# An eight-tile prologue rebuilt: order of transfers, paired conditioning blocks, gate rows as two float32 products side by side

## Chip, cores and metric

One Trainium2 chip, one of its cores. The metric is the device time of the program in microseconds (us), median of its runs. The kernel is written in Bass: every engine has an instruction list of its own and the engines meet at semaphores (`wait_ge`, `then_inc`), so the order on each engine is the order in the code.

## The reference

One layer over x of 1024 tokens by 1024 columns, all float32. What matters here is how it begins:

```
mod = silu(c) @ w_ada + b_ada
shift, scale, gate = split(mod, 3)
h = x * (1 + scale) + shift
proj = h @ w_in + b_in
```

`proj` has 6664 columns: q, k, v, z of eight stick-breaking attention heads of 64, q, k, v, o, z of four mLSTM heads of 128, eight columns of input and forget gates, and two merge gates of 1024 columns. Attention and mLSTM follow, both are projected, merged with the sigmoids of the merge gates, multiplied by `w_out`, and `LayerNorm(alpha * x + (1 + gate) * y)` is the output.

## The kernel before

Products are made in float32r, with each float32 operand split in a high part and a rest (`hH`, `hL`; `wH`, `wL`) and three products for each (`split_product`, L614): high by high, high by low, low by high. h lies transposed in SBUF, eight tiles of 128 columns by 1024 tokens. A *job* (`project`, L621) is 128 output columns for all tokens: eight tiles by two halves of 512 tokens by three products, 48 in all. Five jobs (0 to 4) belong to the prologue, the rest follow in a fixed order under the attention and mLSTM work of four iterations. After the prologue the tensor engine (PE) works through one list to the end.

**The prologue** makes h tile by tile and, as each tile is there, adds its share to jobs 0, 1 and 2 at once: job 0 is the eight gate columns, 1 and 2 are q and k of the first pair of heads. For tile d:

- SyncE (SP) loads x's columns (half a MiB in rows of 512 bytes, L453) and two blocks of `w_ada`, shift and scale (half a MiB each, L457), into one of `A_BUFS` = 3 buffers, and at the first tiles the chunks of `w_in` for the jobs (L443). Seven small loads of parameters stand ahead of all of them (L434, L435).
- VectorE (DVE) sums the eight row blocks of `w_ada` times `silu(c)` (`ada_rows`, L1323: L1331, L1334, L1337).
- The PE sums over the partitions with a product by ones (`ada_columns`, L650; line L655 in the profile); DVE adds the bias (`mod_columns`, L1362).
- The PE transposes x's eight blocks of 128 by 128 (`turn_x`, L659; L667). ScalarE (ACT) makes h from them with scale and shift (`shifted`, L937: L944, two halves) and its high part (L948); DVE makes the rest (`low_h`, L1358).
- The PE makes 18 products for the tile (`tile_of`, L671; lines L617 to L619): six for job 0, whose weights have 8 columns, six for job 1, six for job 2.

The PE's order is: turn of tile d, products of tile d - 1 for jobs 0 and 1, column product of tile d + 1, products of tile d - 1 for job 2. Jobs 3 and 4 follow as ordinary jobs (L639). Job 3 uses the same two PSUM banks as job 1, so its first product waits until ACT has copied out the first half of job 1.

The results of job 0 are copied by ACT (`bias_copy`, L959 to L961), and then SP copies its two groups of rows to four places each, with four small transfers for `r_f` (L470) and four for `r_i` (L472). ACT's exponential (L993) waits for all eight; DVE's scans over the gates (L1388 to L1408) follow, with the splits of weight chunks 9 and on between them (L1343). GpSimd (POOL) only clears buffers in the prologue.

## Time and profile before

| | us |
|---|---|
| median of three runs | 962.69 (962.66 to 962.82) |
| the profiled execution, its own time | 964.36 |
| its span, first to last instruction | 962.6 |
| PE busy | 931.1 (97%) |
| VectorE busy | 616.4 (64%) |
| ScalarE busy | 440.4 (46%) |
| GpSimd busy | 165.5 (17%) |

The span is what the profile's views divide; the run's own time lies 1.7 us above it. Busy time of the PE counts a matmul from its start to its modelled end, so neighbours overlap: how fast the PE works is seen from the distance between starts. Times in the rows are us from the span's start unless they are marked ns.

### The profile page before, as it was taken

To read this page: it belongs to the slowest core of one execution; us is meant where nothing else is said; L and a number is where in the kernel's file an instruction comes from. 1 tells how busy PE (TensorE), PEld (TensorE's weight loads), DVE (VectorE), ACT (ScalarE), POOL (GpSimd) and SP (SyncE) were. 2 spreads that over 40 slices of the span, in tenths; PEclk is the share of its full clock that TensorE was granted. 3 is DMA by queue.
4 is the path that set the end of the run, shared out by engine and by line. 5 is a ranking of instruction groups with operands and counts; after the bars stand their busy time and mean duration, and the time that the engine had idled before them with its cause. 6 is when DMAs were issued, how large, how long until landed. Compare 5 with 4: busy or idle time off the path is not lost.

```text
span 962.6 us, 12901 instructions
## 1 busy us (share of the span) xinstructions
PE 931.1 (97%) x4965; PEld 759.7 (79%) x4965; DVE 616.4 (64%) x1112; ACT 440.4 (46%) x717; POOL 165.5 (17%) x114
## 2 busy tenths in 40 slices
PE   2999999999999999999999999999999999999996
PEld 1677878888878888788888888888888888878885
DVE  4756886755976647976649967534653333345996
ACT  2454566553666544575544665425743222242100
POOL 1010232220223230322311322211100000001200
PEclk9999999999999999999999999999999999999999
DMA  9941211112201022111112111127612212215232
GB/s 228 291 99 48 67 35 39 35 36 67 77 23 45 23 55 78 43 45 34 33 44 89 33 35 34 43 55 237 211 45 67 53 46 53 88 44 186 91 129 87
DMA packets 99560, 73.95 MB, mean 77 GB/s; under 512 B 4616, under 2 KB 90760, under 8 KB 99500
## 3 DMA queue, kind: packets, MB, share of 16 engines
q1 hardware_dynamic: 94828, 58.44, 22.7%
q0 software_dynamic: 2368, 8.41, 2.6%
q10 hardware_dynamic: 2304, 6.29, 1.8%
q8 instruction: 39, 0.64, 0.3%
q14 instruction: 21, 0.17, 0.1%
HBM read 64.59 MB, written 8.40 MB: 76 GB/s over the span
## 4 chain that ended last, share of the span: by engine, by line
PE 89%; DVE 4%; ACT 2%; SPq 2%; DMA 2%; issue 1%; DVEq 0%; ACTq 0%
PE bank L639 44%; PE bank L619 10%; PE bank L617 10%; PE bank L618 10%; PE bank L758 4%; PE bank L746 3%; PE bank L733 2%; DMA a_raw<-in_w_ada 2%; PE bank L716 2%; DVE rem L1503 1%; PE bank L735 1%; PE bank L734 1%; SPq L457 1%; PE bank L781 1%; PE bank L783 1%
## 5 line engine op out<-in xcount | busy, mean ns | idle before, releaser
L639 PE MATMUL bank<-hH,wH 128*128 128x512 f32 x688 | 271.1, 394 | 0.6 <-DVE wL L1343 0.6
L639 PE MATMUL bank<-hL,wH 128*128 128x512 f32 x688 | 271.2, 394 | 0.0
L639 PE MATMUL bank<-hH,wL 128*128 128x512 f32 x688 | 271.1, 394 | 0.0
L577 POOL TENSOR_TENSOR ez<-ez,rem 128x512 f32<-128x512 f32 x72 | 134.5, 1881 | 396.8 <-DVE rem L1503 396.8
L1343 DVE SCALAR_TENSOR_TENSOR wL<-w_raw,wH 128x512 fp32r<-128x512 f32 x116 | 99.3, 860 | 109.2 <-ACT wH L920 107.9
L639 PEld LDWEIGHTS bank<-hH,wH 128*128 128x128 f32 x688 | 129.3, 188 | 30.3 <-DVE wL L1343 2.1
L639 PEld LDWEIGHTS bank<-hH,wL 128*128 128x128 f32 x688 | 129.3, 188 | 28.8 <-issue 2.9
L639 PEld LDWEIGHTS bank<-hL,wH 128*128 128x128 f32 x688 | 129.2, 188 | 28.8 <-issue 2.9
L1503 DVE TENSOR_TENSOR_SCAN rem<-rem,ones 128x512 f32<-128x512 f32 (+2 forms) x96 | 99.9, 1093 | 35.1 <-ACT rem L1020 35.1
L920 ACT ACTIVATE wH<-w_raw 128x512 fp32r<-128x512 f32 x116 | 72.5, 627 | 104.3 <-PE bank L619 71.1
L1008 ACT ACTIVATE ez<-bank 128x512 f32<-128x512 f32 x72 | 39.1, 596 | 101.1 <-PE bank L735 101.1
L618 PE MATMUL bank<-hL,wH 128*128 128x512 f32 x144 | 56.2, 390 | 0.0
L617 PE MATMUL bank<-hH,wH 128*128 128x512 f32 x144 | 56.2, 390 | 0.0
L619 PE MATMUL bank<-hH,wL 128*128 128x512 f32 x144 | 56.0, 389 | 0.0
L606 POOL TENSOR_TENSOR yL<-yT,yH 128x1024 fp32r<-128x1024 f32 x4 | 9.6, 2402 | 207.5 <-ACT yH L1272 207.5
L1016 ACT ACTIVATE rem<-ez 128x512 f32<-128x512 f32 x72 | 41.4, 625 | 7.7 <-DVE y_stage L1510 6.1
L1020 ACT ACTIVATE rem<-rem 128x512 f32<-128x512 f32 x72 | 41.1, 621 | 0.0
L1027 ACT ACTIVATE at<-bank 128x512 f32<-128x512 f32 x72 | 38.7, 592 | 3.3 <-PE bank L746 3.3
L617 PE MATMUL bank<-hH,yH 128*128 128x512 f32 x96 | 38.5, 401 | 0.0
L618 PE MATMUL bank<-hL,yH 128*128 128x512 f32 x96 | 38.1, 396 | 0.0
L619 PE MATMUL bank<-hH,yL 128*128 128x512 f32 x96 | 38.0, 396 | 0.0
L746 PE MATMUL bank<-ident,ez 128*128 128x128 f32 x288 | 37.2, 272 | 0.0
(241 smaller groups left out, 1499.6 us busy)
## 6 DMA issues: line engine op xcount, KB each, us to landing
w_raw<-in_w_in SPq DMA_DIRECT2D x104, 256.0 KB, 2.9
a_raw<-in_w_ada SPq DMA_DIRECT2D x16, 512.0 KB, 7.3
x_rows<-in_x SPq DMA_DIRECT2D x8, 512.0 KB, 6.4
raw<-in_w_ada POOLq DMA_DIRECT2D x8, 512.0 KB, 4.8
x_in<-in_x SPq DMA_DIRECT2D x8, 512.0 KB, 4.2
out_y<-res SPq DMA_DIRECT2D x7, 512.0 KB, 2.9
raw<-in_w_out SPq DMA_DIRECT2D x10, 256.0 KB, 4.5
m_w<-bm_scratch ACTq DMA_DIRECT2D x4, 512.0 KB, 3.5
```

Source lines behind the costliest of these rows:

```text
L577: g.tensor_tensor(e, e, r, ALU.mult).then_inc(a_done[h], 1)
L617: t.matmul(ps, aH, bH, start=k == 0, stop=False)
L618: t.matmul(ps, aH, bL, start=False, stop=False)
L619: return t.matmul(ps, aL, bH, start=False, stop=k == kt - 1)
L639: ins = t.matmul(banks(number)[half][:], w, a, start=(r == 0), stop=(r == JOB_MM // 2 - 1))
L746: ins = t.transpose(z_ps[h][:, b * P:(b + 1) * P], ez[s % 2][h][:, b * P:(b + 1) * P], ident[:])
L920: a.activation(wH[:, slot, :, 0:width], w_raw[:, slot, :, 0:width], ACT.Copy, scale=scale)\
L1008: a.activation(ez[s % 2][h][:], z_ps[h][:], ACT.Exp).then_inc(ex_done[h], 1)
L1016: a.activation(rem[s % 2][h][:], ez[s % 2][h][:], ACT.Ln, bias=1.0).then_inc(ln_done[h], 1)
L1020: a.activation(r, r, ACT.Exp, scale=-1.0).then_inc(rem_done[h], 1)
L1343: v.scalar_tensor_tensor(out=wL[:, slot, :, 0:width], in0=w_raw[:, slot, :, 0:width], scalar=scale, in1=wH[:, slot, :, 0:width], op0=ALU.m ...
L1503: v.tensor_tensor_scan(back, back, ones[:, 0:1].to_broadcast((P, hi - lo)), first, ALU.mult, ALU.min).then_inc(scan_done[h], 1)
```

## The change

The prologue alone is touched, up to the copy of job 0.

- **Order of loads.** SP first issues two small loads (c and `b_ada`), then for each block the conditioning weights, then x. The other five small loads go out from ACT, ahead of its table load. The first three chunks of `w_in` follow block 0, the next three block 3. The parameters are transposed in two parts.
- **Pairs.** Tiles 4 and 5 and tiles 6 and 7 are each one block: two pieces of `w_ada` (half of the rows each) of 256 columns, so rows of 1 KB, and one load of x of 256 columns. There are four buffers for conditioning weights; the fourth lies in the place of `next_v` and `next_g`.
- **Sums ahead.** DVE's order is written out by hand: the sums of the next block are begun before the low part of the tile before.
- **Turns ahead.** The PE transposes x of tile d + 2 behind the products of tile d; column products have places of their own.
- **Gate rows.** Job 0 is no longer three split products. It is one float32 product per half straight from `h_raw`, with unsplit weights (`w_if`), half 0 into partitions 0 to 7 and half 1 into partitions 32 to 39 of one bank. DVE moves half 1 to partitions 0 to 7 before ACT adds the bias.
- **Row copies.** The four loads of `r_i` are issued by ACT between the copies of job 0 and those of job 1; the four of `r_f` stay with SP.

```diff
@@ -127,9 +127,28 @@
-A_BUFS = 3
+A_BUFS = 4
+BLOCKS = [[0], [1], [2], [3], [4, 5], [6, 7]]
+BLOCK_OF = [b for b, tiles in enumerate(BLOCKS) for _ in tiles]
...
+def pro_slot(g):
...
+    return (g // PRO_K) * (PRO_K - 1) + g % PRO_K - 1
...
+def ada_pieces(b):
...
+    if b < 4:
+        return [(b, 0, KT)]
+    return [(2 * b - 4 + part, part * KT // 2, (part + 1) * KT // 2) for part in range(2)]
...
+def ada_freed(number):
...
+    return [KT * b + hi for b in range(len(BLOCKS)) for n, _, hi in ada_pieces(b) if n == number - A_BUFS][0]
@@ -280,13 +300,14 @@
-        a_raw = pt("a_raw", [P, A_BUFS, KT, 2, P])
-        a_acc = pt("a_acc", [P, 2, 2, 2, P])
+        a_raw = [pt(f"a_raw{n}", [P, KT * 2 * P]) for n in range(A_BUFS - 1)] + [next_vg]
+        a_acc = pt("a_acc", [P, 2, 2, 2, 2 * P])
...
+        w_if = pt("w_if", [P, KT, 2 * NH])
@@ -424,17 +458,8 @@
...
+            sp.dma_start(prm[ROW_C:ROW_C + KT, :], c[0].rearrange("(t p) -> t p", p=P)).then_inc(c_in, 16)
+            sp.dma_start(prm[ROW_ADA:ROW_ADA + 3 * KT, :], b_ada[0].rearrange("(t p) -> t p", p=P)).then_inc(c_in, 16)
@@ -448,19 +473,17 @@
-            for d in range(KT):
-                cols_d = slice(d * P, (d + 1) * P)
-                sp.dma_start(x_rows[:, :, cols_d], x_v[:, :, cols_d]).then_inc(x_cols_in[d], 16)
-                if d >= A_BUFS:
-                    sp.wait_ge(ada_used, KT * (d - A_BUFS + 1))
-                for what in range(2):
-                    sp.dma_start(a_raw[:, d % A_BUFS, :, what], w_ada_w[:, :, what, cols_d])\
-                        .then_inc(a_in[d % A_BUFS], 16)
-                if d == 0:
-                    for g in range(3):
-                        pro_load(g)
-                elif d < 4:
-                    pro_load(d + 2)
+            for b, tiles in enumerate(BLOCKS):
+                cols_b = slice(tiles[0] * P, (tiles[-1] + 1) * P)
+                for number, lo, hi in ada_pieces(b):
+                    if number >= A_BUFS:
+                        sp.wait_ge(ada_used, ada_freed(number))
+                    for what in range(2):
+                        sp.dma_start(ada_piece(number, lo, hi)[:, :, what], w_ada_w[:, lo:hi, what, cols_b])\
+                            .then_inc(a_in[number % A_BUFS], 16)
+                sp.dma_start(x_rows[:, :, cols_b], x_v[:, :, cols_b]).then_inc(x_cols_in[b], 16)
+                for g in {0: range(3), 3: range(3, PRO_CHUNKS)}.get(b, ()):
+                    pro_load(g)
@@ -468,8 +491,6 @@
-            for q in range(4):
-                sp.dma_start(r_i[32 * q:32 * q + NH, :], r_if[0:NH, :]).then_inc(rows_in, 16)
@@ -644,42 +665,61 @@
-            pe.wait_ge(params_in, 16 * 7)
-            t.transpose(misc_ps[0][:, 0:P], prm[:], ident[:]).then_inc(m_filled[0], 1)
...
-            def ada_columns(d):
...
-                pe.wait_ge(ada_summed, d + 1)
-                pe.wait_ge(m_drained[0], d + 1)
+            pe.wait_ge(c_in, 16 * 2)
+            r = slice(ROW_ADA, P)
+            t.transpose(misc_ps[0][:, 0:P - ROW_ADA], prm[r, :], ident[r, r]).then_inc(m_filled[0], 1)
+            pe.wait_ge(params_in, 16 * 5)
+            r = slice(0, ROW_ADA)
+            t.transpose(misc_ps[2][:, P:P + ROW_ADA], prm[r, :], ident[r, r]).then_inc(params_turned, 1)
...
+            def ada_columns(b):
...
+                pe.wait_ge(ada_summed, b + 1)
+                if b:
+                    pe.wait_ge(mod_done, b)
+                tiles = len(BLOCKS[b])
...
+                    for n in range(tiles):
+                        ins = t.matmul(ada_ps[:, tiles * what + n:tiles * what + n + 1],
+                                       a_acc[:, b % 2, 0, what, n * P:(n + 1) * P], ones[:, 0:1],
+                                       start=True, stop=True)
...
-                pe.wait_ge(x_cols_in[d], 16)
+                pe.wait_ge(x_cols_in[BLOCK_OF[d]], 16)
...
-                    if n == 0:
-                        pe.wait_ge(mod_done, 2 * d + 2)
-                    elif d:
-                        pe.wait_ge(m_drained[n], d)
+                    if d + 1 - n:
+                        pe.wait_ge(m_drained[n], d + 1 - n)
...
-            def tile_of(k, first, last):
+            def gate_rows(d):
...
+                for n in range(2):
+                    pe.wait_ge(m_drained[n], d + 2 - n)
+                if d % 4 == 0:
+                    pe.wait_ge(wL_done, PRO_K * (d // 4) + 1)
+                for half in range(2):
+                    ins = t.matmul(pro_ps[0][half], w_if[:, d], h_raw[:, d % 2, halves(half)], start=d == 0,
+                                   stop=d == KT - 1, skip_group_check=True)
+                    if d == KT - 1:
+                        ins.then_inc(filled[half], 1)
+                    elif half:
+                        ins.then_inc(if_used, 1)
...
+            def tile_of(k, n):
...
+                g = PRO_K * (k // 4) + n
...
-                    pe.wait_ge(wL_done, PRO_K * (k // 4 + 1))
-                for n in range(first, last):
-                    w = [z[:, PRO_K * (k // 4) + n, k % 4, 0:P if n else 2 * NH] for z in (w_proH, w_proL)]
-                    for half in range(2):
-                        ins = split_product(pro_ps[n][half], w, (hH[:, k, halves(half)], hL[:, k, halves(half)]),
-                                            k, KT)
-                        if k == KT - 1:
-                            ins.then_inc(filled[half], 1)
+                    pe.wait_ge(wL_done, g + 1)
+                w = [z[:, pro_slot(g), k % 4] for z in (w_proH, w_proL)]
+                for half in range(2):
+                    ins = split_product(pro_ps[n][half], w, (hH[:, k, halves(half)], hL[:, k, halves(half)]), k, KT)
+                    if k == KT - 1:
+                        ins.then_inc(filled[half], 1)
@@ -696,16 +736,21 @@
+            turn_x(0)
...
+            turn_x(1)
...
-                turn_x(d)
-                if d:
-                    tile_of(d - 1, 0, PRO_K - 1)
-                if d + 1 < KT:
-                    ada_columns(d + 1)
-                if d:
-                    tile_of(d - 1, PRO_K - 1, PRO_K)
-            tile_of(KT - 1, 0, PRO_K)
+                if d in (1, 2, 5):
+                    ada_columns(min(d + 1, 5))
+                gate_rows(d)
+                if d == 0:
+                    ada_columns(1)
+                tile_of(d, 1)
+                if d == 3:
+                    ada_columns(4)
+                tile_of(d, 2)
+                if d + 2 < KT:
+                    turn_x(d + 2)
@@ -906,6 +951,13 @@
+            bi = b_in[0]
+            for row, src in [(ROW_B, bi[0:OFF_IF]), (ROW_GSB, bi[OFF_GSB:OFF_GSB + 2 * D]), (ROW_CB, conv_b[0]),
+                             (ROW_NG, ml_norm_g[0])]:
+                src = src.rearrange("(t p) -> t p", p=P)
+                act.dma_start(prm[row:row + src.shape[0], :], src).then_inc(params_in, 16)
+            act.dma_start(prm[ROW_CW:ROW_CW + 4 * KT, :], conv_w[0].rearrange("j (t p) -> (j t) p", p=P))\
+                .then_inc(params_in, 16)
@@ -936,8 +990,9 @@
-                act.wait_ge(mod_done, 2 * d + 2)
+                act.wait_ge(mod_done, BLOCK_OF[d] + 1)
...
+                    act.wait_ge(if_used, d - 1)
@@ -977,8 +1034,10 @@
-                        bias_copy(r_if[0:2 * NH, halves(half)], half, n,
-                                  r_bias[0:2 * NH, :], pro_ps[0][half])
+                        else:
+                            act.wait_ge(if_moved, 1)
+                        rows = r_if[0:2 * NH, halves(half)]
+                        bias_copy(rows, half, n, r_bias[0:2 * NH, :], rows if half else pro_ps[0][half])
@@ -988,6 +1047,11 @@
+                if n == 0:
+                    for half in range(2):
+                        act.wait_ge(drained[half], 1)
+                    for q in range(4):
+                        act.dma_start(r_i[32 * q:32 * q + NH, :], r_if[0:NH, :]).then_inc(rows_in, 16)
@@ -1306,36 +1370,45 @@
+            r = slice(ROW_ADA, P)
...
-            def ada_rows(d):
...
+            def other_columns():
+                r = slice(0, ROW_ADA)
+                dve.wait_ge(params_turned, 1)
+                link(v.tensor_copy(cols[:, r], misc_ps[2][:, P:P + ROW_ADA]))
+                link(v.tensor_scalar(cols[:, 0:4], cols[:, 0:4], SB_SCALE, None, ALU.mult))
+                v.tensor_scalar(ncols[:, r], cols[:, r], -1.0, None, ALU.mult).then_inc(params_made, 1)
+                dve.wait_ge(params_made, 1)
...
+            def ada_rows(b, lo, hi):
...
+                if lo == 0 and b > 1:
+                    dve.wait_ge(ada_done, b - 1)
+                for k in range(lo, hi):
+                    for number, first, _ in ada_pieces(b):
+                        if k == first:
+                            dve.wait_ge(a_in[number % A_BUFS], 32 * (number // A_BUFS + 1))
+                    acc, row = ada_sum(b, k % 2), ada_row(b, k)
...
+                if hi == KT:
+                    dve.wait_ge(ada_used, KT * (b + 1))
+                    v.tensor_tensor(ada_sum(b, 0), ada_sum(b, 0), ada_sum(b, 1), ALU.add).then_inc(ada_summed, 1)
@@ -1359,27 +1434,48 @@
-            def mod_columns(d):
-                dve.wait_ge(ada_done, d + 1)
...
-            for d in range(KT):
-                ada_rows(d)
-                if d:
-                    low_h(d - 1)
-                mod_columns(d)
-                if d == 0:
-                    for g in range(3):
-                        pro_split(g)
-                elif d < 4:
-                    pro_split(d + 2)
-            low_h(KT - 1)
+            def mod_columns(b):
+                dve.wait_ge(ada_done, b + 1)
+                first, tiles = BLOCKS[b][0], len(BLOCKS[b])
...
+            other_columns()
+            ada_rows(0, 0, KT)
+            mod_columns(0)
+            for g in range(3):
+                pro_split(g)
+            ada_rows(1, 0, KT // 2)
+            low_h(0)
+            ada_rows(1, KT // 2, KT)
+            ada_rows(2, 0, KT // 4)
+            mod_columns(1)
+            ada_rows(2, KT // 4, KT)
+            low_h(1)
+            mod_columns(2)
+            ada_rows(3, 0, KT)
+            low_h(2)
+            mod_columns(3)
+            ada_rows(4, 0, KT // 2)
+            low_h(3)
+            ada_rows(4, KT // 2, KT)
+            for g in range(3, PRO_CHUNKS):
+                pro_split(g)
+            mod_columns(4)
+            ada_rows(5, 0, KT // 2)
+            low_h(4)
+            ada_rows(5, KT // 2, KT)
+            low_h(5)
+            mod_columns(5)
+            low_h(6)
+            low_h(7)
...
+            dve.wait_ge(filled[1], 1)
+            dve.wait_ge(rows_zero, 5)
+            v.tensor_copy(r_if[0:2 * NH, halves(1)], pro_ps[0][1]).then_inc(if_moved, 1)
```

## Rows read from the trace of the kernel before

**Rows 1.** The page: busy time by engine, and the chain's shares.

```profile
PE 931.1 (97%) x4965; PEld 759.7 (79%) x4965; DVE 616.4 (64%) x1112; ACT 440.4 (46%) x717; POOL 165.5 (17%) x114
...
PE 89%; DVE 4%; ACT 2%; SPq 2%; DMA 2%; issue 1%; DVEq 0%; ACTq 0%
```

**Rows 2.** Stretches: length, PE, PEld, DVE, ACT, POOL busy, granted clock, DMA share, GB/s.

```profile
30.00:40.00 10.00, 9.85 (x54) 6.86 (x52) 7.03 (x19) 5.54 (x7) 0.00 (x0) 1.00 1.17 291
...
40.20:43.60 3.40, 1.88 (x11) 1.56 (x11) 2.80 (x7) 0.00 (x0) 0.00 (x0) 1.00 1.11 286
...
43.60:47.05 3.45, 3.45 (x14) 2.24 (x13) 3.31 (x9) 1.92 (x3) 0.00 (x0) 0.51 1.12 296
...
870.00:880.00 10.00, 10.00 (x45) 8.02 (x44) 4.97 (x9) 5.07 (x7) 4.35 (x2) 1.00 0.97 336
```

**Rows 3.** The chain in order of time: start, length, what.

```profile
29.97 8.32 DMA a_raw<-in_w_ada
...
51.05 0.88 PE bank L667 x8
...
76.09 1.07 ACT r_e L993
```

**Rows 4.** Instructions in order of time: PE, idle time before in brackets.

```profile
41.82 0.61 PE L655 MATMUL bank<-ones,a_acc 128*128 128x1 f32 x4 [1.52 <-DVE a_acc L1337]
...
54.55 0.50 PE L655 MATMUL bank<-ones,a_acc 128*128 128x1 f32 x4
...
60.06 0.50 PE L655 MATMUL bank<-ones,a_acc 128*128 128x1 f32 x4
...
68.35 0.40 PE L617 MATMUL bank<-hH,w_proH 128*128 128x512 f32 x1
...
70.91 0.40 PE L619 MATMUL bank<-hH,w_proL 128*128 128x512 f32 x1
...
71.15 0.39 PE L639 MATMUL bank<-hH,wH 128*128 128x512 f32 x1
...
85.52 0.50 PE L639 MATMUL bank<-hH,wH 128*128 128x512 f32 x1 [0.58 <-DVE wL L1343]
```

**Rows 5.** Instructions in order of time: SyncE, VectorE and ScalarE in the prologue.

```profile
1.27 0.31 SPq L434 DMA_DIRECT2D prm<-in_b_ada  x1
...
3.48 0.43 SPq L453 DMA_DIRECT2D x_rows<-in_x  x1
...
11.43 0.61 DVE L1331 TENSOR_SCALAR a_acc<-a_raw,silu_c 128x256 f32<-128x256 f32 x2 [4.28 <-DMA a_raw<-in_w_ada]
...
66.40 1.89 DVE L1343 SCALAR_TENSOR_TENSOR wL<-w_raw,wH 128x512 fp32r<-128x512 f32 x3
...
67.94 1.28 ACT L961 ACTIVATE r_if<-bank,r_bias 8x512 f32<-8x512 f32 x2 [1.16 <-PE bank L619]
...
69.25 1.39 ACT L961 ACTIVATE next_q<-bank,cols 128x512 f32<-128x512 f32 x2
...
71.92 2.44 SPq L472 DMA_DIRECT2D r_i<-r_if  x4
```

**Rows 6.** Transfers between 870 and 880 us.

```profile
DMA packets 1160, 3.36 MB, mean 336 GB/s; under 512 B 128, under 2 KB 128, under 8 KB 1159
```

**Rows 7.** The chain in order of time: groups of products in two other places.

```profile
129.68 1.06 PE bank L716 x8
...
130.75 1.02 PE bank L758 x16
...
131.77 0.43 PE bank L733 x2
...
863.15 1.72 PE bank L877 x4
```

**Rows 8.** Groups of instructions, 0 to 90 us, shapes apart.

```profile
L944 ACT ACTIVATE h_raw<-bank,mod 128x512 f32<-128x512 f32 x16 | 11.9, 776 | 29.0 <-PE bank L667 29.0
...
L1360 DVE TENSOR_TENSOR hL<-h_raw,hH 128x1024 fp32r<-128x1024 f32 x8 | 9.8, 1222 | 6.6 <-ACT hH L948 6.6
```

More of the change, by code:

```diff
@@ L318, in build_kernel @@
         after.close()
-        params_in, bias_in = sem("params_in"), sem("bias_in")
-        x_cols_in = [sem(f"x_cols_in{d}") for d in range(KT)]
+        c_in, params_in, bias_in = sem("c_in"), sem("params_in"), sem("bias_in")
+        params_turned, params_made = sem("params_turned"), sem("params_made")
+        x_cols_in = [sem(f"x_cols_in{b}") for b in range(len(BLOCKS))]
         a_in = [sem(f"ada_in{n}") for n in range(A_BUFS)]
@@ L378, in build_kernel @@
         M_PRO, M_PER = [10, 9], [20, 20]
-        pro_ps = [[y_ps[0:2 * NH, :], misc_ps[2][0:2 * NH, :]],
+        pro_ps = [[y_ps[32 * half:32 * half + 2 * NH, :] for half in range(2)],
                   [proj_ps[half][:] for half in range(2)], [z_ps[half][:] for half in range(2)]]
-        ada_ps = misc_ps[0]
+        ada_ps = misc_ps[2]
         gate_ps = [y_ps, misc_ps[2]]
@@ L400, in banks, with ada_piece, ada_row, ada_sum @@
             return z_ps if number > J_GATES and (number - J_GATES) % 2 else proj_ps
+        def ada_piece(number, lo, hi):
+            return a_raw[number % A_BUFS][:].rearrange("p (k w c) -> p k w c", k=hi - lo, w=2)
+        def ada_row(b, k):
+            number, lo, hi = [z for z in ada_pieces(b) if z[1] <= k < z[2]][0]
+            return ada_piece(number, lo, hi)[:, k - lo]
+        def ada_sum(b, n):
+            return a_acc[:, b % 2, n, :, 0:len(BLOCKS[b]) * P]
         def gate_buffer(n):
@@ L924, in pro_split @@
                 if g < PRO_CHUNKS:
-                    n = g % PRO_K
-                    columns = P if n else 2 * NH
+                    n, q = g % PRO_K, g // PRO_K
                     act.wait_ge(w_in_s[g % 3], 16 * (g // 3 + 1))
-                    a.activation(w_proH[:, g, :, 0:columns], w_raw[:, g % 3, :, 0:columns], ACT.Copy,
-                                 scale=SB_SCALE if n == 1 else 1.0).then_inc(wH_done, 1)
+                    if n:
+                        dst, part = w_proH[:, pro_slot(g)], w_raw[:, g % 3]
+                    else:
+                        dst, part = w_if[:, 4 * q:4 * q + 4], w_raw[:, g % 3, :, 0:2 * NH]
+                    a.activation(dst, part, ACT.Copy, scale=SB_SCALE if n == 1 else 1.0).then_inc(wH_done, 1)
                     return
@@ L979, in _ @@
                             act.wait_ge(rows_zero, 5)
[L980 to L981 removed]
+                        else:
+                            act.wait_ge(if_moved, 1)
+                        rows = r_if[0:2 * NH, halves(half)]
+                        bias_copy(rows, half, n, r_bias[0:2 * NH, :], rows if half else pro_ps[0][half])
                     elif n < 4:
@@ L1349, in pro_split @@
                     n = g % PRO_K
-                    columns = P if n else 2 * NH
                     dve.wait_ge(wH_done, g + 1)
-                    v.scalar_tensor_tensor(out=w_proL[:, g, :, 0:columns], in0=w_raw[:, g % 3, :, 0:columns],
-                                           scalar=SB_SCALE if n == 1 else 1.0, in1=w_proH[:, g, :, 0:columns],
-                                           op0=ALU.mult, op1=ALU.subtract).then_inc(wL_done, 1)
+                    if n:
+                        v.scalar_tensor_tensor(out=w_proL[:, pro_slot(g)], in0=w_raw[:, g % 3],
+                                               scalar=SB_SCALE if n == 1 else 1.0, in1=w_proH[:, pro_slot(g)],
+                                               op0=ALU.mult, op1=ALU.subtract).then_inc(wL_done, 1)
+                    else:
+                        dve.sem_inc(wL_done, 1)
                 else:
@@ L1381, in _ @@
+            low_h(3)
+            ada_rows(4, KT // 2, KT)
+            for g in range(3, PRO_CHUNKS):
+                pro_split(g)
+            mod_columns(4)
[6 more added lines that the diff above has]
+            low_h(7)
             for g in range(PRO_CHUNKS, PRO_CHUNKS + 3):
                 pro_split(g)
+            dve.wait_ge(filled[1], 1)
+            dve.wait_ge(rows_zero, 5)
```

49 lines of the change are left out of this document (15 added, 34 removed).

## The prediction

> **What bounds the kernel now.** The page comes first: the tensor engine (PE) is busy 97% of the span and makes up 89% of the chain that ended last [rows 1]. From there on only the prologue is of interest, since every edit lies in it; I read it in stretches, then its chain of waits in order of time, then its queues and the durations of its operations.
>
> In the stretches the reader is to see two regimes. Up to about 42 us the transfers bound: in 30 to 40 us they move 291 GB/s with the engines full, while the PE works because it has tiles in stock [rows 2]. The chain says the same: it runs over the landing of a conditioning block, 8.32 us from 29.97 on, and then over VectorE's sums [rows 3]. After that the PE never waits: column products of neighbouring tiles start 5.51 us apart (54.55 and 60.06) [rows 4]. The last product of tile 7 starts at 70.91 and the first product of the next job at 71.15 [rows 4]. **71.15 us is the mark** against which I hold the change; I call its place after the change E. The rows of the gates come behind it: eight small transfers from one queue, an exponential at 76.09, and at 85.52 a PE that has waited 0.58 us for a split on VectorE [rows 3 to 5].
>
> One more thing is in the stretches: between 40.2 and 43.6 us the PE was busy 1.88 of 3.40 us, waiting 1.52 us for the sums of tile 4 [rows 2, 4], and from 43.6 to 47.05 its granted clock was 0.51, the lower of its two levels (1.2 against 2.4 GHz). That costs half of 3.45 us, 1.7 us, and is in the 71.15.
>
> **The change, part by part.**
>
> *Start.* Seven small transfers stand ahead of the first x transfer, which SyncE issues at 3.48 us; two remain, the second issued at 1.27 for 0.31 us, so the large ones begin at about 1.6 us, 1.9 us sooner [rows 5]. The five others go out on ScalarE's queue, ahead of its table load: about 5 x 0.3 us. They delay the silu of c to about 5 us and the new columns of parameters to about 6 us; the first conditioning block can't be there before 7.5 us, which hides both. If those small transfers landed 5 us late, the sums would start 3 us late, and the wait for data further on would absorb that too.
>
> *Supply.* Now 1 MiB of conditioning weights and then half a MiB of x go per tile. 1.5 MiB (x and weights of tile 0) were there at 11.4 us [rows 5], after the change at 9.5. At 291 GB/s a MiB takes 3.60 us. Up to and with the six w_in chunks, 7.03 MiB pass: 9.5 + 5.53 x 3.60 = 29.4 us. Then come 2 MiB of weights and 1 MiB of x for tiles 4 and 5, in packets of 1 KB instead of 512 B. No row has that size. One bound is 291 GB/s; the other the stretch 870 to 880 us, 336 GB/s at a share of 0.97 with packets of 2.9 KB in the mean (3.36 MB in 1160) [rows 2, 6], or 346 GB/s full. A straight line through time per packet (28 ns at 512 B, 134 ns at 2.9 KB) gives 51 ns for 1 KB, 322 GB/s, 3.26 us per MiB; I take that. Bounds for 3 MiB: 9.1 and 10.8 us. x of tile 4 then lands at 39.2 us (38.5 to 40.8 with the bounds and 0.6 us either way on the start).
> The Trainium skill (DMA: Bandwidth & Descriptors, Specifications) gives 512 B as the least transfer for line rate. By that rule the pairs gain nothing and x of tile 4 lands at 40.2 us. The rows speak against it.
>
> *Who waits for it.* "x turned two tiles ahead" puts the turn of tile 4 behind the products of tile 2 and ahead of the gate rows of tile 3. PE's own work gets there by about 36.5 us: x of tile 1 lands at 9.5 + 2.03 x 3.60 = 16.8, then come three turns (2.6), three column products (1.4), three tiles (11.7, below) and some 4 us for the lower clock at the start. So it waits 2.7 us for x of tiles 4 and 5, which lands behind both pieces of the weights. Weights first thus make the sums early and this turn late.
>
> *From that landing to E.* PE work: four turns (4 to 7) at 0.88 us [rows 3], 3.5; column products of both pairs at 0.8 (one tile's take 5.51 - 18 x 0.2325 - 0.88 = 0.45, these have twice as many), 1.6; five tiles (3 to 7) with twelve products 0.2325 us apart (68.35 to 70.91 in eleven steps [rows 4]), 2.79, and gate rows. Gate rows were six products, 1.39 us. Now they are two full float32 products of 512 columns. One alone is two passes of 0.43 us (four in 1.72) [rows 7]. Two outputs in different groups of columns run side by side in this trace: sixteen passes of 128 columns took 1.02 us, 0.064 each, where one alone takes 0.11 (turns: eight in 0.88 [rows 3]). So 0.86 us, plus two switches of the array's form: the stretch of eight turns before those passes took 1.06 instead of 0.88, and two products after them 0.43 instead of 0.23; I take 1.1. Bounds 0.95 and, if the two don't run side by side, 1.95. Five tiles: 5 x 3.89 = 19.5. Waits: the chain column product, mod, h (two copies of 0.78), its high half, its low half (1.22) [rows 8] shows through at tile 4 by about 1.3 us. Sum 3.5 + 1.6 + 19.5 + 1.3 = 25.9. E = 39.2 + 25.9 = **65.1, which is 6.0 us ahead of 71.15**. VectorE isn't late: a sum over 512 columns is at most the 0.63 us of a split of that width [rows 5], nine for a pair 5.7 us, and the last end with the PE still on tile 4.
>
> *The clock.* 1.52 us of waiting was followed by 3.45 us at the lower level. I expect a lower clock again, for as long, a part of it inside the wait: 1.4 us lost (0, where it stays up, to 3.4, where it stays down twice as long).
>
> *The new wait at E.* Four of the eight small row transfers move from SyncE to ScalarE, between the copies of job 0 and those of job 1. On SyncE one takes 0.58 us, four 2.44 [rows 5]. Before, ScalarE went from the copies of job 0 (67.94, 1.28 us) straight to those of job 1 at 69.25 [rows 5], and the first product of job 3 needs the first half of job 1 copied. After: gate rows end at E - 2.65; the second half is moved down by VectorE, behind its three splits (1.89 us [rows 5]), to E - 1.45; ScalarE copies it to E - 0.7, issues four transfers to E + 1.75, copies half 0 of job 1 (0.69), and the PE starts job 3 at E + 2.5. **A wait of 2.5 us** (1.5 to 2.7) takes the place of none. The same fall of the clock behind it: 1.2 us (0 to 1.7).
>
> *The gate rows' chain.* Eight transfers in two queues take the time of four; ScalarE is at the exponential at E + 4.5 instead of E + 4.9, and the PE is 2.5 us later. The wait of 0.58 us before 85.52 goes: -0.6.
>
> Sum: -6.0 + 1.4 + 2.5 + 1.2 - 0.6 = **-1.5 us**. The profiled run (964.36 us, span 962.6) becomes 962.9; it stands 1.7 us above the median, so the median becomes 961.2. What a measurement of this kernel can tell from no change is 0.2%, 1.9 us; the forecast lies inside it, near its lower edge.
>
> **The rivals.**
>
> *The clock holds, or the wait at E is short.* The PE has more queued work ahead of both waits than it had at 40 us. Without either fall: -6.0 + 2.5 - 0.6 = -4.1, 958.6 us. For it: E is bound by supply, and that is 1.9 us earlier for sure. Against: behind the wait that ended at 41.82 the clock did fall.
>
> *Slower: the turn of tile 4 waits too long.* Place: the turn ahead of tile 3's gate rows. Price: with the pairs at 291 GB/s x lands at 40.8, the PE waits over 4 us, and the clock stays low twice as long as in [rows 2], 6.9 us (3.0 lost, the rest of it in the wait). E = 66.7, then +3.0 + 2.5 + 1.7 - 0.6: +2.2 us, 964.9 us. It decides from a landing of about 40.5 us on, with both falls of the clock.
>
> *Gate rows don't run side by side.* The groups that do in this trace are 64 columns wide, these take 8 each. 0.85 us more on five tiles, about one hidden: +3.2 on the forecast, +1.7 in all, 964.4 us.
>
> *The change doesn't do what it says:* 1 KB packets move no faster and nothing else: 1.0 us more, -0.5, 962.2 us.
>
> **How the numbers follow.** Forecast with its near variants (one fall of the clock), within 0.2%: 0.40. The change doesn't do what it says, within 0.2%: 0.03. Clock holds or wait short, faster by over 0.2%: 0.41. The two slower cases: gate rows 0.04, of which half stays within 0.2%; long wait 0.12. So faster 0.41, same 0.45, slower 0.14. The range leaves out the ends of all bounds taken together: 957.3 to 964.7.
>
> **What would show it.** Right: first sums at about 7.5 us; a wait of 2 to 4 us of the PE for x at about 36 to 39; granted clock at the lower level behind it; gate row passes in pairs, 0.43 us apart; the first product of job 3 2 to 3 us behind the last of tile 7, released by ScalarE, with four transfer issues ahead of that copy; no wait at the ninth chunk. Wrong: no wait for x (supply was misjudged), job 3 starting without a gap, or a mark above 71.15 from something outside the prologue.

## The result, and the profile after

| us | before | after |
|---|---|---|
| median, runs taken with the comparison | 962.76 (962.20 to 963.45, 20 runs) | 964.03 (963.28 to 964.84, 20 runs) |
| profiled execution, its own time | 964.36 | 963.45 |
| its span | 962.6 | 961.7 |
| mean granted clock of it | 0.996 | 0.994 |
| start of the last product of tile 7 | 70.91 | 68.15 |
| first product of job 3 (the mark) | 71.15 | 70.98 |

The ratio is 1.0013 [1.0007, 1.0019]: 1.3 us slower, inside what I called no change and inside the range, but not the 1.5 us faster that was forecast. The two profiled executions give the other sign, 0.9 us faster. That contradiction is the first thing to explain.

The page of the kernel after, busy time and shares of the chain [rows 1]:

```profile
PE 931.5 (97%) x4950; PEld 757.5 (79%) x4950; DVE 614.5 (64%) x1085; ACT 440.0 (46%) x717; POOL 165.5 (17%) x114
...
PE 90%; DVE 3%; ACT 3%; DMA 2%; SPq 1%; issue 1%; ACTq 0%; DVEq 0%
```

It looks like the page before, fifteen products fewer. The change is in the order, so the stretches are read next (columns as in [rows 2]):

```profile
30.00:40.00 10.00, 6.40 (x34) 4.38 (x32) 9.01 (x15) 3.79 (x7) 0.00 (x0) 0.93 1.10 349
40.00:48.00 8.00, 7.93 (x31) 5.31 (x32) 2.14 (x6) 0.81 (x2) 0.00 (x0) 0.66 1.11 343
38.57:45.39 6.82, 5.32 (x16) 3.01 (x17) 2.52 (x4) 0.00 (x0) 0.00 (x0) 0.50 1.10 348
```

The transfers move 349 GB/s where they moved 291, yet the tensor engine (PE) is busy 6.40 of 10 us where it was busy 9.85. The last row is the whole stretch at the lower clock: 6.82 us, of which the PE worked 5.32, so half of that, 2.7 us, is lost. Before it was 3.45 us, all of it with work. The PE is idle for the first 1.5 us of the stretch: its wait for x began at 36.40 us and ended at 40.07, and the clock fell at 38.57.

PE in order of time (idle time before in brackets):

```profile
16.83 1.97 PE L694 MATMUL bank<-ident,x_rows 128*128 128x128 f32 x8 [4.38 <-DMA x_rows<-in_x]
40.07 1.97 PE L694 MATMUL bank<-ident,x_rows 128*128 128x128 f32 x8 [3.67 <-DMA x_rows<-in_x]
49.27 1.03 PE L705 MATMUL bank<-h_raw,w_if 128*8 128x512 f32 x4
51.10 0.50 PE L638 MATMUL bank<-hH,w_proH 128*128 128x512 f32 x1 [0.79 <-DVE hL L1435]
68.15 0.40 PE L640 MATMUL bank<-hH,w_proL 128*128 128x512 f32 x1
70.98 0.47 PE L660 MATMUL bank<-hH,wH 128*128 128x512 f32 x1 [2.43 <-ACT next_q L1018]
```

Two waits carry the story: 3.67 us for x ahead of the turn of tile 4, and 2.43 us for ScalarE ahead of job 3. Between them there is one short wait. ScalarE (ACT) in order of time shows what stands behind the second:

```profile
65.66 0.68 ACT L1018 ACTIVATE r_if<-bank,r_bias 8x512 f32<-8x512 f32 x1 [1.18 <-PE bank L705]
66.73 0.72 ACT L1018 ACTIVATE r_if<-r_if,r_bias 8x512 f32<-8x512 f32 x1 [0.39 <-DVE r_if L1478]
67.54 2.56 ACTq L1054 DMA_DIRECT2D r_i<-r_if  x4
70.15 1.26 ACT L1018 ACTIVATE next_q<-bank,cols 128x512 f32<-128x512 f32 x2 [2.70 <-issue]
73.67 1.06 ACT L1057 ACTIVATE r_e<-r_f 128x1024 f32<-128x1024 f32 x1 [1.10 <-DMA r_f<-r_if]
```

Four issues of 0.64 us each stand ahead of the copy that job 3 waits for, as forecast. Last, what the main queue had moved by the landing of x of tile 1 and by that of tiles 4 and 5 (queue, packets, MB, share; the windows 0 to 16.79 and 0 to 40.03 us):

```profile
q1 hardware_dynamic: 8361, 3.95, 94.8%
...
q1 hardware_dynamic: 19552, 11.24, 106.2%
```

### The profile page after: what moved, and what is told of

It is laid out like the page before. It is cut to its first block, busy times and chain, and to the rows that moved or that the text cites. A ratio compares the mean times of both kernels' runs of the same rounds, so it can differ in the third digit from the quotient of the medians.

```text
span 961.7 us, 12860 instructions
## 1 busy us (share of the span) xinstructions
PE 931.5 (97%) x4950; PEld 757.5 (79%) x4950; DVE 614.5 (64%) x1085; ACT 440.0 (46%) x717; POOL 165.5 (17%) x114
## 4 chain that ended last, share of the span: by engine, by line
PE 90%; DVE 3%; ACT 3%; DMA 2%; SPq 1%; issue 1%; ACTq 0%; DVEq 0%
PE bank L660 46%; PE bank L638 9%; PE bank L640 9%; PE bank L639 9%; PE bank L803 4%; PE bank L791 3%; DMA x_rows<-in_x 2%; PE bank L778 2%; PE bank L761 2%; DVE rem L1599 1%; PE bank L780 1%; PE bank L779 1%; PE bank L826 1%; PE bank L828 1%; PE bank L815 1%; PE bank L823 1%
## 5 line engine op out<-in xcount | busy, mean ns | idle before, releaser
L638 PE MATMUL bank<-hH,yH 128*128 128x512 f32 x96 | 38.5, 401 | 0.0
```

The lines of the kernel that those rows point to most:

```text
L638: t.matmul(ps, aH, bH, start=k == 0, stop=False)
```

## The experiments

The theory after the result (A): the profiled execution of the kernel before held a fall of the clock that its usual executions don't have; the change gained some microseconds of supply and gave them back in its two waits. The rivals: another part of the change costs time outside the prologue; the wait for x is the transfers' own limit and can't be removed.

**1. The kernel before, again** (no edit).

> The kernel before, unchanged. Question: is the fall of the granted clock at 43.6 us, which cost 1.7 us in its profiled execution (span 962.6 us, mean clock 0.996), there in its usual executions (median 962.76)? Theory A (it is not; the profiled execution was 1.6 us above the median for this reason): most executions have a mean clock of about 0.998 and spans near 961.0 us, the odd one 0.996 and 962.6. Theory B (it is; profiled executions are longer for another reason): mean clock 0.996 in all, whatever the time.

Measured: 962.69 us (962.47 to 963.07, 11 runs); profiled execution 962.76, span 961.0. PE in order of time:

```profile
41.31 0.61 PE L655 MATMUL bank<-ones,a_acc 128*128 128x1 f32 x4 [0.16 <-DVE a_acc L1337]
...
69.43 0.39 PE L639 MATMUL bank<-hH,wH 128*128 128x512 f32 x1
...
83.89 0.50 PE L639 MATMUL bank<-hH,wH 128*128 128x512 f32 x1 [0.68 <-DVE wL L1343]
```

and the stretch that stood at 0.51 in [rows 2]:

```profile
43.60:47.05 3.45, 3.45 (x21) 2.41 (x20) 3.42 (x9) 2.51 (x3) 0.00 (x0) 1.00 1.17 290
```

The same program waits 0.16 us where it had waited 1.52 [rows 4], the clock stays up, and the mark lies at 69.43, 1.72 us ahead of 71.15. Of the 1.72 us, 1.6 are the fall: from this column product to the next (49.03 and 46.91 us) it is 7.21 us with the fall and 5.60 without. The sums were also ready 0.5 us sooner, and 0.4 us was lost again further on. What differs ahead of that is when the clock first rose, 29.5 us here and 26.6 in the first profiled execution. A slower start fills a wait that is there anyway for the sums; that this decides about the fall fits all three profiled executions of this order (experiment 7 has the third), but no run forces it.

Which of the two is usual is told by the mean clocks and the times: 0.997 or 0.998 in all 75 runs of the kernel before that were timed beside my experiments, and none above 963.64 us (962.21 to 963.64), against 0.996 and 964.36 us in the first profiled execution. **The mark of the usual kernel before is about 69.4, not 71.15.** The marks also settle one rival: from the mark to the end of the span, less the wait at the ninth chunk, it is 890.9 us in both profiled executions of the kernel before and 890.7 in that of the kernel after. Nothing is lost outside the prologue.

**2. The r_i transfers from GpSimd's queue** (all else as after):

```diff
-                if n == 0:
-                    for half in range(2):
-                        act.wait_ge(drained[half], 1)
-                    for q in range(4):
-                        act.dma_start(r_i[32 * q:32 * q + NH, :], r_if[0:NH, :]).then_inc(rows_in, 16)
...
+            for half in range(2):
+                pool.wait_ge(drained[half], 1)
+            for q in range(4):
+                pool.dma_start(r_i[32 * q:32 * q + NH, :], r_if[0:NH, :]).then_inc(rows_pool, 16)
...
```

> The changed kernel with the four r_i row transfers issued by GpSimd instead of ScalarE; nothing else moves. Theory A (ScalarE's four issues, 2.56 us, between the copies of job 0 and job 1 hold up job 3): ScalarE goes from the copy of job 0 to that of job 1 at once, the wait of 2.43 us before job 3 goes, the time falls by about 2.4 us, and by a further 1 us in the median if the fall of the clock behind that wait made half of the executions longer: 960.5 to 961.5 us. Theory B (job 3 would wait anyway, for its weight chunks or the late copy of the second half of the gate rows): under 1 us gained.

Measured: 962.13 us (961.50 to 962.88, 11 runs), ratio to before 0.9994 [0.9985, 1.0003]; 1.9 us less than after. Job 3 starts at 67.40 without a wait, and a new one stands at the ninth weight chunk:

```profile
82.65 0.50 PE L666 MATMUL bank<-hH,wH 128*128 128x512 f32 x1 [1.46 <-DVE wL L1418]
```

The wait of 2.43 us is gone. Between the profiled executions 3.6 us were won at the mark, 2.4 of them from that wait; most of the rest is not the edit's, since the low clock lasted 3.41 us here, 2.9 of them under work, against 5.3 in the kernel after. Then 1.5 us were given back 15 us later: the next time at which something must be ready is VectorE's split of chunk 9, behind both scans. The expectation had missed that wait, and its 960.5 to 961.5 us with it.

**3. x ahead of the weights** (for the two pairs, `x_rows` is loaded ahead of both pieces of `a_raw`):

```diff
+                if b > 3:
+                    sp.dma_start(x_rows[:, :, cols_b], x_v[:, :, cols_b]).then_inc(x_cols_in[b], 16)
                 for number, lo, hi in ada_pieces(b):
...
-                sp.dma_start(x_rows[:, :, cols_b], x_v[:, :, cols_b]).then_inc(x_cols_in[b], 16)
+                if b < 4:
+                    sp.dma_start(x_rows[:, :, cols_b], x_v[:, :, cols_b]).then_inc(x_cols_in[b], 16)
```

> The changed kernel with x of each pair loaded ahead of the pair's conditioning weights; ScalarE's issues stay. Theory A (x of tiles 4 and 5, 40.03 us, held up the turn of tile 4 and with it the products of tile 3; the 3.7 us of waiting brought the clock down for 6.8 us): x lands near 34 us, the turn doesn't wait, the wait moves to the column product of tile 4 and is about 2 us, the last product of tile 7 comes 3 us sooner (about 65.3), the time falls by 3 us to about 961 us. Theory B (the supply of the weights bounds in either order): the sums of tiles 4 and 5 come 2.9 us later, and what the turn gains the column product loses; within 1 us of the changed kernel's 964.0.

Measured: 963.47 us (961.90 to 966.03, 11 runs), 1.0013 [1.0005, 1.0022] against before. The profiled execution is one of the long ones (965.52 us): its clock was down for 10.24 us from 40.92 on. The wait for x is gone, and one as long has taken its place:

```profile
40.38 0.50 PE L641 MATMUL bank<-hH,w_proH 128*128 128x512 f32 x1 [4.23 <-DVE hL L1438]
43.76 1.87 PE L686 MATMUL bank<-ones,a_acc 128*128 128x1 f32 x8 [0.89 <-DVE a_acc L1414]
71.44 0.58 PE L663 MATMUL bank<-hH,wH 128*128 128x512 f32 x1 [2.44 <-ACT next_q L1021]
71.82 0.63 PE L663 MATMUL bank<-hL,wH 128*128 128x512 f32 x1
```

VectorE's order is written out by hand, and the low part of tile 3 stands behind the first half of the sums of tiles 4 and 5, whose weights now come later. In order of time:

```profile
36.94 0.94 DVE L1407 TENSOR_SCALAR a_acc<-a_raw,silu_c 128x512 f32<-128x512 f32 x2 [6.36 <-DMA a_raw<-in_w_ada]
37.79 1.41 DVE L1410 SCALAR_TENSOR_TENSOR a_acc<-a_raw,silu_c,a_acc 128x512 f32<-128x512 f32 x2
39.11 1.22 DVE L1438 TENSOR_TENSOR hL<-h_raw,hH 128x1024 fp32r<-128x1024 f32 x1
```

A DVE that waits 6.36 us for weights holds back work that needs none of them: the high part of tile 3 was there at 33.2 us. The product of 0.63 us behind job 3's wait (0.40 at the full clock) belongs to a further fall of the clock, from 71.64 to 75.05.

**4. Edits 2 and 3 together.**

> Both edits: r_i rows by GpSimd and x of a pair ahead of its weights. If the two waits are separate, the gains add: 964.0 - 2.4 - 3 gives 958.0 to 959.5 us, below the kernel before (962.76). If one only covers for the other (the rows' chain becomes late and VectorE's scans hold up the ninth weight chunk), about half of that: 960.5 us.

Measured: 962.48 us (960.79 to 963.61, 11 runs), 0.9993 [0.9984, 1.0002]. The profiled execution is one of the quick ones (960.98) and waits 4.90 us for the low part of tile 3 and 1.40 at the ninth chunk. No gain over edit 2 alone (962.13): with VectorE's order as it stands, x first is not the remedy. These runs fall into two groups, five of 960.8 to 961.8 at mean clocks of 0.995 to 0.996 and six of 962.5 to 963.6 at 0.992 to 0.993; how long the clock stays down around the long wait differs between executions (3.41 us in this profiled one, 10.24 in that of experiment 3).

**5. The turn of tile 4 later** (as after; the turn goes behind tile 3's products for job 1 and the column product of tiles 4 and 5):

```diff
                 tile_of(d, 1)
                 if d == 3:
                     ada_columns(4)
+                    turn_x(4)
                 tile_of(d, 2)
-                if d + 2 < KT:
+                if d + 2 < KT and d != 2:
                     turn_x(d + 2)
```

> The changed kernel with one move: the turn of tile 4 goes behind the products of tile 3 for job 1 and the column product of tiles 4 and 5, and no longer stands ahead of tile 3's gate rows. Theory A (the place of the turn): tile 3's 2.4 us of work fill the time until x has landed at 40.0 us; the tensor engine waits 1.1 us for the sums of tiles 4 and 5 (ready at 39.9) instead of 3.7 us for x, and about 0.4 us more for tile 4's halves. The last product of tile 7 ends 2.6 us sooner with the clock as it was, up to 5.3 us sooner if it no longer falls: between 63.1 and 65.8 us against 68.4. The wait of 2.4 us ahead of job 3 stays. Median 959 to 961.5 us against 964.0. Rival B (the transfers bound): x of tiles 6 and 7 can't be there before 49.5 us, and 13.8 us of work stand behind it, so 63.3 us is the floor; within A's range, it would show as a wait for x at 48 us. Rival C (the wait only moves, as it did when x was fetched ahead of the weights): 963 us or more.

Measured: 960.79 us (959.01 to 961.40, 11 runs), 0.9977 [0.9968, 0.9986] against before: 3.2 us less than after (2.2 between the profiled executions). PE in order of time:

```profile
36.23 0.50 PE L638 MATMUL bank<-hH,w_proH 128*128 128x512 f32 x1 [1.26 <-DVE hL L1436]
40.66 1.86 PE L683 MATMUL bank<-ones,a_acc 128*128 128x1 f32 x8 [2.76 <-DVE a_acc L1412]
...
68.76 0.47 PE L660 MATMUL bank<-hH,wH 128*128 128x512 f32 x1 [2.50 <-ACT next_q L1019]
```

The two waits add up to 4.0 us, against 3.67 and 0.79 in the kernel after, but tile 3 is done between them and no wait for tile 4's low part follows, and the mark is 2.2 us ahead though the clock was down as long (40.22 to 47.04). The wait for sums is 2.76 us, not 1.1: their last one ended at 40.6, not at 39.9. There is no wait for x at 48 us either, so the transfers aren't the limit yet.

**6. Chunk 9's split between the scans** (on edit 2):

```diff
                 v.tensor_tensor_scan(r_b[:], r_one[:], r_f[:], 0.0, ALU.mult, ALU.add).then_inc(dve_step, 1)
                 link.k += 1
+                pro_split(PRO_CHUNKS + 3)
                 link(v.tensor_tensor_scan(r_m[:], r_f[:], r_i[:], 0.0, ALU.add, ALU.max))
...
             row_logs()
-            pro_split(PRO_CHUNKS + 3)
             row_columns()
```

> The kernel with the r_i transfers on GpSimd's queue (962.1 us), with one move on VectorE: the low part of weight chunk 9 is made between the two scans over the gate rows instead of behind both. Theory A: the tensor engine's wait of 1.46 us at 82.65 goes entirely, since the split ends 2.3 us sooner; 960.7 us. Rival: the high part on ScalarE or the transfer of the chunk is what comes last; then the wait stays at over 1 us and the time at 962. A second rival: the second scan, 0.6 us later, makes the gate columns late for their turn 23 us behind the start of job 3; a wait of up to 0.6 us there, 961.3 us.

Measured: 960.99 us (960.63 to 963.79, 11 runs), 0.9986 [0.9977, 0.9995] against before, 1.1 us less than edit 2. The wait of 1.46 us is gone and the second rival's has come, 0.70 us for the gate columns:

```profile
90.13 1.09 PE L737 MATMUL bank<-ident,r_q 128*128 128x128 f32 x8 [0.70 <-ACT r_q L1066]
```

**7. The same split in the kernel before.**

> The kernel before, with chunk 9's low part made between the two scans. In it the tensor engine waits 0.68 us at 83.89 for that split. Theory A: the wait goes, 962.0 us against 962.7, and no more. Rival: the wait is for something else that comes at the same time; then no difference. This says how much of the earlier place of tile 7 any kernel with the scans first can keep: in the changed kernel the split ends at 83.04, 0.8 us ahead of before, though its last tile ended 1.1 us ahead.

Measured: 962.14 us (961.69 to 963.56, 11 runs), 0.9993 [0.9984, 1.0002] against before, 0.55 us less: the size forecast, though the interval doesn't exclude none. Its profiled execution is the slowest of its runs (963.56, clock 0.996) and waits 1.42 us for the sums of tile 4 and has the clock down from 43.57 to 46.98, as the first profiled execution of before had, and its clock first rose at 26.5 us, as there; the ten others have 0.997 or 0.998 and lie between 961.7 and 962.4. Here too the execution with the fall lies 1.4 us above the median of those that by their mean clock had none.

**8. The three edits together** (2, 5 and 6 on after).

> All three edits of the changed kernel together: turn of tile 4 later, r_i on GpSimd's queue, chunk 9's low part between the scans. If the three waits are what the kernel loses and they add: job 3 starts at 63.3 to 65.8 us against 69.4 in the kernel before, no wait at the ninth chunk, median 956.5 to 959.5 us. Rival: x of tiles 6 and 7 is waited for at 48 us, the clock falls again behind that wait, and 1 to 3 us are given back: 959 to 961. If another due time stands behind (gate columns, weight chunks 10 and on), a new wait appears between 75 and 95 us.

Measured: 958.08 us (957.51 to 959.76, 5 runs), 0.9956 [0.9944, 0.9969] against before: 4.6 us faster than before and 6.0 faster than after. PE in order of time:

```profile
40.60 1.16 PE L689 MATMUL bank<-ones,a_acc 128*128 128x1 f32 x8 [2.68 <-DVE a_acc L1414]
...
64.64 0.39 PE L666 MATMUL bank<-hH,wH 128*128 128x512 f32 x1
...
87.40 1.09 PE L737 MATMUL bank<-ident,r_q 128*128 128x128 f32 x8 [0.81 <-ACT r_q L1067]
```

The medians add up: 1.9 us for the queue of r_i, 1.1 for the split behind it and 3.2 for the turn alone make 6.2, and all together gave 6.0. What is left is the wait of 2.68 us for the sums of tiles 4 and 5, 0.75 for the low part of tile 3 ahead of it, and 0.81 at the gate columns.

**9. The r_i transfers back on SyncE** (that part of the change undone).

> The changed kernel with the four r_i transfers back on SyncE behind the four of r_f, as in the kernel before: this part of the change undone. Theory A: they cost the wait of 2.4 us ahead of job 3 on ScalarE's queue, and on SyncE's queue they cost the gate rows next to nothing, since the exponential started 6.2 us behind the copies with ScalarE's queue, 6.8 with GpSimd's and 7.0 in the kernel before, with all eight on SyncE. So it is the GpSimd version within 0.3 us: job 3 without a wait, a wait of 1.5 to 1.8 us at the ninth chunk, 962.3 us against 964.0. Rival: eight transfers in one queue make the gate rows 2.5 us later; then the wait at the ninth chunk is 4 us and the time 964.6, the change's own.

Measured: 962.12 us (961.67 to 963.15, 11 runs), 0.9997 [0.9988, 1.0006] against before. PE in order of time:

```profile
40.12 1.97 PE L696 MATMUL bank<-ident,x_rows 128*128 128x128 f32 x8 [6.15 <-DMA x_rows<-in_x]
...
67.61 0.39 PE L662 MATMUL bank<-hH,wH 128*128 128x512 f32 x1
...
82.99 0.50 PE L662 MATMUL bank<-hH,wH 128*128 128x512 f32 x1 [1.60 <-DVE wL L1413]
```

Job 3 starts without a wait, the wait at the ninth chunk is 1.60 us, and the time that of edit 2. So undoing this one part takes 1.9 us from the change, and the change without it is 0.6 us faster than before by the medians (not more than the interval allows). The rival is out: with all eight transfers in one queue the exponential starts 6.9 us behind the last copy of `r_if`, with GpSimd's help 6.8. What ended its wait here was the landing of `r_i`, which it doesn't read; no run lets it wait for the four of `r_f` alone.

**10. The pairs' transfers in packets of 512 bytes** (each load of 256 columns made as two of 128, the waits raised to match; for x):

```diff
-                sp.dma_start(x_rows[:, :, cols_b], x_v[:, :, cols_b]).then_inc(x_cols_in[b], 16)
+                for n in tiles:
+                    cols_n = slice(n * P, (n + 1) * P)
+                    sp.dma_start(x_rows[:, :, cols_n], x_v[:, :, cols_n]).then_inc(x_cols_in[b], 16)
```

> The changed kernel with every transfer of the pairs split in two by columns, so that its packets have 512 bytes again; all else stays. It prices the packets of 1 KB, which moved 349 GB/s where those of 512 bytes moved 290. Theory A (the larger packets carry the gain in supply): 3 MiB take 10.8 us instead of 9.0, x of tile 4 is there at 41.8 us instead of 40.0, the tensor engine's wait for it grows from 3.7 to 5.4 us, job 3 starts 1.8 us later, at 72.8, and the clock stays down no shorter: 965.8 us (965.3 to 967.5). Rival (from 512 bytes on the packet size changes nothing, the rate of 349 GB/s came with the stretch): 964.0 us, x at 40.0.

Measured: 966.17 us (965.34 to 966.41, 5 runs), 1.0033 [1.0021, 1.0046] against before, 2.1 us more than after. The stretches 30 to 40 us and 72.77 to 76.19:

```profile
30.00:40.00 10.00, 6.39 (x34) 4.37 (x32) 7.10 (x12) 3.77 (x7) 0.00 (x0) 0.93 1.16 291
...
72.77:76.19 3.42, 3.42 (x10) 2.64 (x9) 0.00 (x0) 2.23 (x4) 0.00 (x0) 0.50 0.73 156
```

and PE in order of time:

```profile
41.96 1.97 PE L698 MATMUL bank<-ident,x_rows 128*128 128x128 f32 x8 [5.57 <-DMA x_rows<-in_x]
...
72.10 0.47 PE L664 MATMUL bank<-hH,wH 128*128 128x512 f32 x1 [2.45 <-ACT next_q L1022]
```

The same loads in the same order move 291 GB/s instead of 349, and the turn is 1.89 us later. The mark is only 1.1 us later, since more of the low clock now lies inside the wait. The rest of the span's 2.7 us is a second fall of the clock, behind job 3's wait: the second row of the stretches. The median is 2.1 us above after's. So it is the size of the packets that carries the gain in supply. The Trainium skill (DMA: Bandwidth & Descriptors, Specifications) puts line rate at transfers of 512 bytes or more; the traces disagree, 291 against 349 GB/s for 512 and 1024 bytes in the same stretch, and the measurement decides. That a fall can follow the wait at job 3 is shown here and in experiment 3; the profiled execution of the kernel after has the same wait and no fall.

## Why the prediction was wrong, step by step

All marks and spans of this section are those of profiled executions.

**The step that failed: "it stands 1.7 us above the median, so the median becomes 961.2".** I had read the cause of these 1.7 us myself, at the start of the prediction: a fall of the clock worth 1.7 us "is in the 71.15". The sum compared a changed kernel, with a fall of its own priced in, with a mark that held before's fall, and so counted its absence as gain; then 1.7 us were subtracted a second time to come to the median. An execution without the fall is the usual one (experiments 1 and 7), so the sum's own -1.5 us meant +0.1 against the median (-1.5 plus the 1.6 us between 964.36 and 962.76). That alone takes the whole forecast gain away. The other 1.2 us of the measured +1.3 are 0.6 from the terms below (the spans differ by -0.9, forecast -1.5) and 0.6 by which after's median lies above its profiled execution.

**The terms of the sum**, against the profiled execution:

| term | forecast | measured |
|---|---|---|
| x of tiles 4 and 5 landed | 39.2 | 40.03 |
| work from there to E, without the clock | 25.9 | 25.7 |
| clock at 40 us | +1.4 | +2.7 |
| wait at E, with the clock behind it | +2.5, +1.2 | +2.6, 0 |
| wait at the ninth chunk | -0.6 | -0.6 |
| sum | -1.5 | -0.8 (spans: -0.9) |

- *Start and supply.* x of tile 1 landed at 16.79 us (forecast 16.8). The rate of 1 KB packets was 349 GB/s, above my 322 and about at the bound of 346; that is 0.8 us sooner over 3 MiB. It was more than lost in the landing: by 16.79 the queue had moved 3.95 MB = 3.77 MiB where 3.53 were needed, by 40.03 11.24 MB = 10.72 MiB where 10.03 were. So 0.69 instead of 0.24 MiB of later loads had gone ahead of x's last bytes, at 3.0 us per MiB 1.3 us. Some 0.2 us more went between 26 and 28 us, where the transfers moved 255 GB/s instead of 290. Why the lag is larger for the load of 1 MiB isn't shown; the amounts are. Two bounds were also uneven: the 38.5 leaves out the 0.6 us that its upper partner has, and the 40.8 of the long-wait rival has it on top of the 40.2 that 291 GB/s give. Neither decided anything.
- *The turn of tile 4* waited as forecast in place and cause, 3.67 instead of 2.7 us, the 0.8 us of the landing. Experiment 5 shows that its place, with the supply as it is, costs 3.2 us.
- *Work to E.* 28.35 us from 40.03 to 68.38 (the start of the last product and its 0.23), less 2.66 for the clock. Gate rows ran side by side: the four passes at 49.27 take 1.03 us by the record, where four alone took 1.72 [rows 7], and they start in two pairs 0.43 us apart; at tile 5 (55.74) it is 0.96 us to the next product. The rival is out. One wait for tile 4's low part, 0.79 us, for the 1.3 forecast.
- *The clock.* This is the term that was most mis-sized: the fall lasted 6.82 us, twice as long as before's, with 5.32 us of it under work, so 2.7 us lost where 1.4 was the term and "3.4, where it stays down twice as long" the bound. Other executions of the same order up to here lost less: in experiment 2 it was down 3.41 us and cost 1.4, in experiment 9 6.83 us, but with only 3.45 under work, and cost 1.7. Their last product of tile 7 starts at 67.17 and 67.38, not at 68.15. What a fall costs depends on how much of it lies inside the wait, and that differs between executions of one order.
- *The wait at E* was 2.43 us and all of ScalarE's four issues, as forecast; the fall behind it isn't in the profiled execution, but in those of experiments 3 and 10. Of the 20 runs of after, ten lie between 963.3 and 964.0, ten between 964.1 and 964.8 us, and the eight at mean clocks of 0.992 or 0.993 are all in the second half; none of the 22 runs of experiments 2 and 9, which have no wait at E, is below 0.994. That the second half holds this fall is likely and not shown: none of them was profiled, and the runs of experiment 2 spread nearly as widely (961.50 to 962.88) without that wait. Whatever the cause, after's median is 0.6 us more than its profiled time.
- *The ninth chunk.* Its wait went, as forecast, though the exponential came 5.3 us behind E (73.67 against 68.38) and not 4.5. The reason caps the change: the split behind the scans ends at 83.84 us in the kernel before (experiment 1) and at 83.04 after, 0.8 us sooner, though tile 7 ended 1.1 us sooner. Take the wait at E away, and this one is next (experiments 2, 9).

From the result back: -0.9 us in spans, +0.6 to after's median, +1.6 from before's profiled execution to its median: +1.3, the measured difference.

**Of the rivals**, the long wait had named place and mechanism, and it decided: the clock down for 6.82 us, with a landing at 40.03, ahead of the 40.5 from which I let it decide, and with the faster packets that it denied. Its 964.9 us is near the 964.0 measured by luck: it too was counted from 71.15 and then set on the median, and without that slip it says 966.5. The clock held in one of the two places, at E, and not at 40 us, so the faster case didn't come. Gate rows one after the other and pairs without effect are out.

All the signs that the prediction lists for "right" came, nearly in size (first sums at 7.93 us, the two waits, the low clock, the pairs of passes, the four issues, no wait at the ninth chunk). They test the mechanism of the kernel after. None of them tests the base that it was compared with, and there the error lay.

## What to carry to other kernels

Before a sum is made on one profiled execution, ask what sets it apart from the median; a clock fall that the median's runs lack may be counted in the base or in the step to the median, not in both. An operation put early in a queue "ahead of need" is a wait for everything behind it, as soon as its data are late: put it where the engine still has work that doesn't need it. And the issues of small transfers belong on a queue that nothing waits for: here ScalarE's four cost 1.9 us of the median. After each wait removed, look at once for the next time at which something must be ready (here the split of chunk 9).

## What the runs showed that I had not expected

- The time at which the clock first rose lay anywhere between 19.6 and 29.5 us in these profiled executions, and it hardly moved the end: in experiment 9 it rose at 19.7, the PE stood in front of the turn of tile 4 for 6.15 us, and the turn began at 40.12; in experiment 2 it rose at 26.0, the wait was 3.31, the turn at 40.19. A wait for data takes up what the clock gives. The Trainium skill (TensorE: Matmul & The Clock Gate, What you observe) says that the point at which the clock rises varies by 0.5 us either way between runs. These traces agree that it varies, and by more: 26.6 and 29.5 us in the two of the kernel before. In the three profiled executions of the kernel before's order the early rises (26.5 and 26.6) go with a later wait of 1.4 to 1.5 us and a fall, the late one with 0.2 us and none.
- Eight small transfers on one queue cost the gate rows hardly more than two queues of four: the exponential starts 6.2 us behind the last copy of `r_if` with four on ScalarE's queue (73.67 against 66.73 + 0.72), 6.8 with four on GpSimd's, 6.9 with all on SyncE's (experiment 9).
- The packets' rate, 291 GB/s at 512 bytes and 349 at 1 KB, both with the transfer engines full (shares of 1.16 and 1.10): the second is above the 322 that a straight line between the neighbouring rows gave.
